# Final RMSNorm of a one-layer decoder: squares and norm weights handled per output block, last two blocks by token halves

## The reference

```python
def rmsnorm(x, g):
    xf = x.astype(jnp.float32)
    y = xf * lax.rsqrt(jnp.mean(xf * xf, axis=-1, keepdims=True) + EPS)
    return (y * g.astype(jnp.float32)).astype(x.dtype)
...
y = jnp.concatenate([ssm_out, att_out], axis=-1) @ w_out
...
y_prompt = rmsnorm(hp, g_final)[:, N_META:]
y_sample = rmsnorm(hs, g_final)
```

## Time and profile before

| what | value |
|---|---|
| median of 3 runs | 1257.17 us (1252.75 to 1259.44) |
| the profiled execution's own time | 1260.12 us |
| its span, first to last instruction | 1258.4 us |
| mean granted TensorE clock | 0.946 of full |
| busy: PE, DVE, ACT, POOL | 90%, 47%, 30%, 10% |
| last transpose of the projection ends | 1237.0 us |
| first write of `o_y_p` issued | 1244.1 us |
| write of `o_y_s` issued | 1255.6 us |

### The profile page before, as it was taken

How to read it: one execution, slowest core, us unless ns; L and a number is a source line. 1 busy time by engine, 2 the same in 40 slices (tenths; PEclk the granted TensorE clock), 3 DMA queues, 4 the chain that set the end, 5 groups by cost and what they waited for, 6 DMA issues and landing times.

```text
span 1258.4 us, 25162 instructions
## 1 busy us (share of the span) xinstructions
PE 1128.7 (90%) x9906; PEld 1032.3 (82%) x9906; DVE 585.2 (47%) x1205; ACT 375.0 (30%) x622; POOL 120.8 (10%) x192
## 2 busy tenths in 40 slices
PE   3899949999999999596989997799999988999993
PEld 3799949999999999586989975566666648999992
DVE  5843513442588521384646363455555462232224
ACT  6311101111233222335422213444444351121213
POOL 0000110000000000003405301022223100000000
PEclk8799969999999999698989898899999999999996
DMA  9343491332343532415437656166777728323203
GB/s 265 85 126 102 119 145 43 86 85 85 94 125 102 143 103 82 101 47 180 126 92 218 201 179 212 34 194 194 214 213 220 203 76 266 105 67 100 84 17 135
DMA packets 197187, 165.70 MB, mean 132 GB/s; under 512 B 35195, under 2 KB 163478, under 8 KB 195270
## 3 DMA queue, kind: packets, MB, share of 16 engines
q1 hardware_dynamic: 176358, 118.08, 33.4%
q0 software_dynamic: 9696, 27.04, 8.0%
q10 hardware_dynamic: 11048, 19.41, 4.6%
HBM read 139.36 MB, written 22.78 MB: 129 GB/s over the span
## 4 chain that ended last, share of the span: by engine, by line
PE 80%; DVE 6%; DMA 5%; ACT 3%; issue 3%; SPq 1%; POOL 0%; ACTq 0%; DVEq 0%
PE gemm L1758 13%; PE gemm L1760 13%; PE gemm L1759 13%; PE gemm L2084 5%; PE gemm L2086 4%; PE gemm L2085 4%; PE misc L1997 4%; PE gemm L2037 3%; PE gemm L2016 2%; DMA w_raw<-w_out 1%; PE misc L1834 1%; PE misc L1841 1%; PE misc L1983 1%; PE misc L1785 1%; PE gemm L1947 1%
## 5 line engine op out<-in xcount | busy, mean ns | idle before, releaser
L1758 PE MATMUL gemm<-xh,w_hi 128*128 128x260 f32 (+2 forms) x1120 | 321.9, 287 | 0.2 <-DVE w_lo L1152 0.2
L1760 PE MATMUL gemm<-xh,w_lo 128*128 128x260 f32 (+2 forms) x1120 | 319.8, 286 | 0.0
L1759 PE MATMUL gemm<-xl,w_hi 128*128 128x260 f32 (+2 forms) x1120 | 319.5, 285 | 0.0
L1152 DVE TENSOR_TENSOR w_lo<-w_raw,w_hi 128x2048 fp32r<-128x2048 f32 (+3 forms) x65 | 113.6, 1748 | 259.8 <-ACT w_hi L787 258.8
L1758 PEld LDWEIGHTS gemm<-xh,w_hi 128*128 128x128 f32 x1120 | 212.2, 189 | 1.1 <-DVE w_lo L1152 0.4
L1759 PEld LDWEIGHTS gemm<-xl,w_hi 128*128 128x128 f32 x1120 | 212.3, 190 | 0.0
L1760 PEld LDWEIGHTS gemm<-xh,w_lo 128*128 128x128 f32 x1120 | 212.1, 189 | 0.0
L787 ACT ACTIVATE w_hi<-w_raw 128x2048 fp32r<-128x2048 f32 (+3 forms) x63 | 90.7, 1439 | 354.7 <-PE gemm L1760 339.4
L2084 PE MATMUL gemm<-comb_hi,w_hi 128*128 128x260 f32 x512 | 147.4, 288 | 3.9 <-DVE w_lo L1642 2.9
L2086 PE MATMUL gemm<-comb_hi,w_lo 128*128 128x260 f32 x512 | 145.4, 284 | 0.0
L2085 PE MATMUL gemm<-comb_lo,w_hi 128*128 128x260 f32 x512 | 145.4, 284 | 0.0
(11 more groups left out here) (340 smaller groups left out, 1949.1 us busy)
## 6 DMA issues: line engine op xcount, KB each, us to landing
w_raw<-w_in SPq DMA_DIRECT2D x35, 1024.0 KB, 6.0
ckv<-cache_ckv POOLq DMA_DIRECT2D x72, 256.0 KB, 3.5
w_raw<-w_out SPq DMA_DIRECT2D x16, 1024.0 KB, 5.9
ckv<-cache_ckv SPq DMA_DIRECT2D x56, 256.0 KB, 2.9
z_d<-ev ACTq DMA_DIRECT2D x16, 260.0 KB, 2.1
w_raw<-w_glu SPq DMA_DIRECT2D x8, 512.0 KB, 4.4
yt<-x_prompt SPq DMA_DIRECT2D x4, 1024.0 KB
o_y_p<-yt SPq DMA_DIRECT2D x4, 1024.0 KB
```

The lines of the kernel that those rows point to most:

```text
L1152: dve.tensor_tensor(w_lo[:, slot, 0:width], w_raw[:, slot, 0:width], w_hi[:, slot, 0:width].bitcast(F32), ALU.subtract).then_inc(w_lo_read ...
L1758: pe.matmul(acc, a, xa, start=k == 0, stop=False)
L1759: pe.matmul(acc, a, xb, start=False, stop=False)
L1760: last = pe.matmul(acc, b, xa, start=False, stop=k == k_tiles - 1)
```

## The change

Five things are done:

1. Blocks 0 to 13: after a block is added, ACT squares its 128 columns in each of the five token tiles, each with an accumulated sum into a column of a new table `parts` (5 tiles by 16), and DVE then multiplies these columns of `yt` and `ysm` by their norm weights (`square_block`, `out_gain`). The sums are of the values ahead of the norm weights.
2. ACT takes a square root of a constant column ahead of the projection's copies.
3. Blocks 14 and 15 are multiplied, copied, turned and added by token halves, in the order 14 first half, (turn of block 13), 15 first half, 15 second half, 14 second half, with the turns of finished halves set between groups of contraction tiles.
4. The norm has two parts: token tiles 0 and 1 after the first halves of blocks 14 and 15 are added, under the second halves' matmuls; tiles 2, 3 and the sample tokens at the end. In a part ACT squares only the last 256 columns of each tile; DVE sums the 15 partial sums of its tiles in one instruction, and mean, root and reciprocal are made once for the part.
5. The scale goes onto the first 1792 columns, which hold their norm weights already, by a multiplication with one scalar per token: by ACT for tiles 1, 3 and the sample tokens (`y_scaled`), by DVE for 0 and 2. The last 256 columns are done as before, by scale and norm weights together. SP waits for both.

The diff, cut to its core:

```diff
@@ -204,6 +204,7 @@
         gfin = at("gfin", A0 + 57344, [P, D_MODEL])
         yb = at("yb", A0 + 65536, [P, 2, SEQ + N_SAMPLE])
         junk2 = at("junk2", A0 + 69696, [P, D_MODEL])
+        parts = at("parts", C0 + 1024, [P, 5, 16])
         oh = at("oh", A0, [P, 2, V_HEAD])
         zas = at("zas", A0 + 4096, [P, N_HEADS, N_SAMPLE])
         oz = at("oz", A0 + 4352, [P, N_HEADS, N_SAMPLE])
@@ -344,6 +345,7 @@
         out_t_ready = sem("out_t_ready")
         out_added = sem("out_added")
         y_stored = sem("y_stored")
+        y_scaled = sem("y_scaled")
         comb_hi_done = sem("comb_hi_done")
         comb_lo_done = sem("comb_lo_done")
 
@@ -404,6 +406,7 @@
         RING = len(ckv)
         S_BANK, SC, PVS, TP, PVB = (gemm[0], gemm[1]), gemm[2], gemm[3], misc[0], misc[1]
         T_BANK = (misc[2], misc[3])
+        MAIN = 14 * P
         EXTRA = slice(496, 512)
         NM, SM, SME, RS, PARTS = 24, 32, 40, 48, 56
 
@@ -690,10 +693,14 @@
                 for u in range(2):
                     sp.wait_ge(w_lo_ready, i * 2 + (B_OUT + 1 + u))
                     load_out(i * 2 + (2 + u), u)
+            o_y = d["o_y_p"].rearrange("b s m -> (b s) m")
             for t in range(4):
                 sp.wait_ge(x_scaled, t + 6)
-                sp.dma_start(d["o_y_p"].rearrange("b s m -> (b s) m")[t * P:(t + 1) * P, :], yt[:, t, :]).then_inc(y_stored, 16)
+                if t % 2:
+                    sp.wait_ge(y_scaled, t // 2 + 1)
+                sp.dma_start(o_y[t * P:(t + 1) * P, :], yt[:, t, :]).then_inc(y_stored, 16)
             sp.wait_ge(x_scaled, 10)
+            sp.wait_ge(y_scaled, 3)
             sp.dma_start(d["o_y_s"].rearrange("b s m -> (b s) m"), ysm[0:N_SAMPLE, :]).then_inc(y_stored, 16)
             sp.wait_ge(y_stored, 16 * 5)
 
@@ -1111,18 +1118,57 @@
 
             act.wait_ge(os_step, 6)
             act.activation(comb_hi[:, 8:16, T_PROMPT:T], oz[:], ACT.Copy).then_inc(os_step, 1)
-            with act.Fori(0, 7) as i:
+            act.activation(stat[:, 63:64], ident[:, 0:1], ACT.Sqrt)
+
+            def out_tile(t):
+                return (yt[:, t], P) if t < 4 else (ysm[0:N_SAMPLE], N_SAMPLE)
+
+            def squares(tiles, cols, width, col):
+                for t in tiles:
+                    y, rows = out_tile(t)
+                    last = act.activation(junk2[0:rows, t * 2 * P:t * 2 * P + width], y[:, cols], ACT.Square,
+                                          accum_out=parts[0:rows, t, col])
+                last.then_inc(x_squared, 1)
+
+            def square_block(j):
+                act.wait_ge(out_added, j + 3)
+                act.wait_ge(x_squared, j + 5)
+                squares(range(5), ds(j * P, P), P, ds(j, 1))
+
+            def out_copy_half(j, slot, h, done):
+                act.wait_ge(gemm_done, done)
+                act.wait_ge(out_t_ready, j + 1)
+                act.activation(yb[:, slot, h * 260:(h + 1) * 260], gemm[2 * slot + h][:, 0:260], ACT.Copy).then_inc(gemm_read, 1)
+
+            def finish(part, tiles, full):
+                act.wait_ge(out_added, 18 + 2 * part)
+                act.wait_ge(x_squared, 19 + part)
+                squares(tiles, slice(MAIN, D_MODEL), 2 * P, slice(14, 15))
+                act.wait_ge(var_ready, 8 + part)
+                act.activation(stat[:, 16:16 + len(tiles)], stat[:, 8:8 + len(tiles)], ACT.Sqrt).then_inc(std_ready, 1)
+                act.wait_ge(rstd_ready, 8 + part)
+                for t in full:
+                    y, rows = out_tile(t)
+                    at_t = 24 + t - tiles[0]
+                    act.activation(y[:, 0:MAIN], y[:, 0:MAIN], ACT.Copy, scale=stat[0:rows, at_t:at_t + 1]).then_inc(y_scaled, 1)
+
+            for u in range(2):
+                out_copy(u, u)
+                out_hi(2 + u, u, 1)
+            square_block(0)
+            with act.Fori(0, 6) as i:
                 for u in range(2):
-                    out_copy(i * 2 + u, u)
-                    out_hi(i * 2 + (2 + u), u, i + 1)
-            out_copy(14, 0)
-            out_copy(15, 1)
-            for t in range(5):
-                y, rows = (yt[:, t], P) if t < 4 else (ysm[0:N_SAMPLE], N_SAMPLE)
-                act.wait_ge(out_added, 18)
-                act.activation(junk2[0:rows], y, ACT.Square, accum_out=stat[0:rows, t:t + 1]).then_inc(x_squared, 1)
-                act.wait_ge(var_ready, t + 8)
-                act.activation(stat[0:rows, 16 + t:17 + t], stat[0:rows, 8 + t:9 + t], ACT.Sqrt).then_inc(std_ready, 1)
+                    out_copy(i * 2 + (2 + u), u)
+                    out_hi(i * 2 + (4 + u), u, i + 2)
+                    square_block(i * 2 + (1 + u))
+            DONE = B_V + 14
+            out_copy_half(14, 0, 0, DONE + 1)
+            square_block(13)
+            out_copy_half(15, 1, 0, DONE + 2)
+            finish(0, (0, 1), (1,))
+            out_copy_half(15, 1, 1, DONE + 3)
+            out_copy_half(14, 0, 1, DONE + 4)
+            finish(1, (2, 3, 4), (3, 4))
 
         @block.vector
         def _(dve):
@@ -1696,23 +1742,59 @@
             dve.wait_ge(os_step, 7)
             tt(comb_lo[:, 8:16, T_PROMPT:T], oz[:], comb_hi[:, 8:16, T_PROMPT:T].bitcast(F32), ALU.subtract).then_inc(os_step, 1)
 
+            dve.memset(parts[:], 1.0)
             dve.sem_inc(out_added, 2)
             dve.wait_ge(res_loaded, 16 * 6)
-            with dve.Fori(0, 7) as i:
+
+            def out_gain(j):
+                dve.wait_ge(x_squared, j + 6)
+                cols = yt[:, :, ds(j * P, P)]
+                tt(cols, cols, gfin[:, ds(j * P, P)].unsqueeze(1).to_broadcast([P, 4, P]), ALU.mult)
+                cols = ysm[0:N_SAMPLE, ds(j * P, P)]
+                tt(cols, cols, gfin[0:N_SAMPLE, ds(j * P, P)], ALU.mult)
+
+            def out_add_half(j, slot, h, turned):
+                dve.wait_ge(out_t_ready, turned)
+                cols = yt[:, 2 * h:2 * h + 2, j * P:(j + 1) * P]
+                last = tt(cols, cols, misc[slot][:, 2 * h * P:(2 * h + 2) * P].rearrange("p (t n) -> p t n", t=2), ALU.add)
+                if h:
+                    cols = ysm[0:N_SAMPLE, j * P:(j + 1) * P]
+                    last = tt(cols, cols, misc[2 + slot][0:N_SAMPLE, 0:P], ALU.add)
+                last.then_inc(out_added, 1)
+
+            def finish(part, tiles, full):
+                n = len(tiles)
+                dve.wait_ge(x_squared, 20 + part)
+                dve.reduce_sum(stat[:, 0:n], parts[:, tiles[0]:tiles[-1] + 1, 0:15], axis=AX.X).then_inc(comb_step, 1)
+                dve.wait_ge(comb_step, 9 + part)
+                dve.tensor_scalar(stat[:, 8:8 + n], stat[:, 0:n], 1.0 / D_MODEL, EPS, ALU.mult, ALU.add).then_inc(var_ready, 1)
+                dve.wait_ge(std_ready, 8 + part)
+                dve.reciprocal(stat[:, 24:24 + n], stat[:, 16:16 + n]).then_inc(rstd_ready, 1)
+                dve.wait_ge(rstd_ready, 8 + part)
+                for t in tiles:
+                    y, rows = (yt[:, t], P) if t < 4 else (ysm[0:N_SAMPLE], N_SAMPLE)
+                    scale_t = stat[0:rows, 24 + t - tiles[0]:25 + t - tiles[0]]
+                    if t in full:
+                        dve.tensor_scalar(y[:, 0:MAIN], y[:, 0:MAIN], scale_t, None, ALU.mult)
+                    dve.scalar_tensor_tensor(out=y[:, MAIN:D_MODEL], in0=y[:, MAIN:D_MODEL], scalar=scale_t, in1=gfin[0:rows, MAIN:D_MODEL],
+                                             op0=ALU.mult, op1=ALU.mult).then_inc(x_scaled, 1)
+
+            for u in range(2):
+                out_lo(2 + u, u)
+                out_add(u, u)
+            out_gain(0)
+            with dve.Fori(0, 6) as i:
                 for u in range(2):
-                    out_lo(i * 2 + (2 + u), u)
-                    out_add(i * 2 + u, u)
-            out_add(14, 0)
-            out_add(15, 1)
-            for t in range(5):
-                y, rows = (yt[:, t], P) if t < 4 else (ysm[0:N_SAMPLE], N_SAMPLE)
-                dve.wait_ge(x_squared, t + 6)
-                dve.tensor_scalar(stat[0:rows, 8 + t:9 + t], stat[0:rows, t:t + 1], 1.0 / D_MODEL, EPS, ALU.mult, ALU.add).then_inc(var_ready, 1)
-                dve.wait_ge(std_ready, t + 8)
-                dve.reciprocal(stat[0:rows, 24 + t:25 + t], stat[0:rows, 16 + t:17 + t]).then_inc(rstd_ready, 1)
-                dve.wait_ge(rstd_ready, t + 8)
-                dve.scalar_tensor_tensor(out=y, in0=y, scalar=stat[0:rows, 24 + t:25 + t], in1=gfin[0:rows],
-                                         op0=ALU.mult, op1=ALU.mult).then_inc(x_scaled, 1)
+                    out_lo(i * 2 + (4 + u), u)
+                    out_add(i * 2 + (2 + u), u)
+                    out_gain(i * 2 + (1 + u))
+            out_add_half(14, 0, 0, 17)
+            out_gain(13)
+            out_add_half(15, 1, 0, 18)
+            finish(0, (0, 1), (0,))
+            out_add_half(15, 1, 1, 19)
+            out_add_half(14, 0, 1, 20)
+            finish(1, (2, 3, 4), (2,))
 
         @block.tensor
         def _(pe):
```

(31 more changed lines are left out.)

## The result

| | kernel before | changed kernel |
|---|---|---|
| median, first comparison (11 runs each) | 1257.17 us | 1249.45 us (1245.53 to 1253.44) |
| ratio, 95% interval | | 0.9936, 0.9920 to 0.9952 |
| median, second comparison (11 and 8 runs) | 1257.56 us | 1249.60 us (1247.18 to 1255.17) |
| ratio, 95% interval | | 0.9924, 0.9908 to 0.9940 |
| span of the profiled execution | 1258.4 us | 1246.8 us |

By the ratios the changed kernel is faster by 0.64% and 0.76%, some 8 and 9.6 us; the medians differ by 7.7 and 8.0 us. The second lies clear of 0.995 too, while the first reaches 0.9952. The forecast was 1248.2, a ratio of 0.9929, in a range of 1244.5 to 1252.6.

What follows compares the result with a forecast made beforehand. PE held 80% of the chain, but mostly DVE the last 20.4 us. First end-part write 2.2 us earlier plus 6.8 less behind it: 9.0 off 1260.12, 1251.1; less 2.95 for the median, 1248.2; range 1244.5 to 1252.6.

Steps and rivals of the forecast that it cites:

- the tail: Stretch from the start of ACT's copy of block 13 to the end of the span; predicted 9.0 us less.
- Loop covered: Projection loop: added squares (1.9 us a block) and weight multiplications hide under matmuls; period stays 12.08 us.
- Halves give nothing by themselves in PE's order: Blocks 14 and 15: end part's squares begin at 1237.94 against 1237.97; the worth is what runs early.
- Part two: End norm of tiles 2, 3 and sample tokens: squares 1.46 us, reciprocal done 1240.27, tile 2 issued 1241.85.
- Writes: Last two large writes: 2.6 us per 1 MB after a 0.65 start, then 1.7 from last data to end.
- The slack of 1.6 us in part one: ACT is ready for its copy of block 15's second half early; 1.6 us remain before PE would wait.
- load 1.3: End chain: moving the table load ahead of the projection makes the first end-part write 1.3 us earlier.
- The rival in which the load stays: A table load ahead of a root in each norm part: 1.3 us more at the end, 1249.5; chance 0.07.
- drain of 1.38 us for each table switch: At the norm's table load: by the skill's drain 1.4 us more gain; left out, as the trace doesn't show it.
- rivals of a stall: PE waits for ACT in part one: stall plus 1.5 us of lost clock costs 4.4, giving 1252.6; chance 0.08.
- overrun loop: ACT's squares set the loop period: 13 blocks each lose 1.0 us and 1.5 by clock, about 1281; chance 0.03.
- the second rival: The overrun loop, where ACT's squares set the period and lost clock is added: about 1281; chance 0.03.

Runs made afterwards that it cites:

- late-ACT kernel: Changed kernel with two more squares of 1792 columns on ACT in part one, results unused; from block 13's copy to the end 39.11 us, 0.97 more.
- long fill: Changed kernel with idle ACT copies of 12288 columns in each of 12 loop periods; 14.23 us a period, 40.5 us from block 13's copy to the end.

## Why the prediction was right

The forecast held, and so did its mechanism: the tail was to shrink by 9.0 us and shrank by 8.81. That the medians agree so well is in part luck: whole times scatter by several us ahead of the tail, and the median of three runs that I started from, 1257.17, happens to be that of all eleven. Step by step, with times from the squares of the end part on:

- **Loop covered.** Shown: the period is unchanged, and unchanged with 4.4 us more on ACT (8.4 of 12.08 us); with 14.2 us of work ACT sets it. Where between these it turns wasn't measured. The squares took 1.56 us a block, not 1.9, since the next square overlaps the read before it.
- **Halves give nothing by themselves in PE's order.** Shown: squares at 26.58 us of the tail against 26.52. I had it at 26.49, 0.03 us earlier than before; of the 0.09 us missing, 0.07 are in PE's matmuls and early transposes and 0.02 in the copy, turn and add.
- **Part two.** Scaling begins after 2.22 us (predicted 2.33), tile 2 is issued after 3.79 (3.91), the sample rows after 5.76 (5.71). DVE's multiplication by one scalar took 1.15 us for 1792 columns, the low end of the bound and what the row's slope gave. ACT's took 1.79 against 1.68: the form that I took the slope from reads no scalar from SBUF. The late-ACT kernel's squares of 1792 columns, which read none either, took 1.68.
- **Writes.** From tile 2's issue to the end 7.77 us (predicted 7.55), at 397 to 422 GB/s. The last window makes 143 GB/s x 2.8 us = 0.40 MB behind 1244.0, about 0.95 us at 422 GB/s, so by this estimate it is 1.85 us from the last data to the end, where I took 1.7. Squares 0.09 later, issue 0.12 sooner behind them and writes 0.22 longer make the 0.19 us missing from 9.0.
- **The slack of 1.6 us in part one.** Measured 1.55. The late-ACT kernel used it up, and PE waited for the rest.

The step that was mis-sized is the load of the table, "load 1.3" in the list of steps. Alone it costs the end 1.04 us (the first root comes 1.09 earlier without it), since it covered DVE's mean, and in the changed kernel it needn't be moved ahead at all. The sum for part two had the mean in the chain already, which is why it came out. The rival in which the load stays was priced with a load in each part; even without the early root there is only one, in part one, and the tail is 0.07 longer.

The drain of 1.38 us for each table switch, which the Trainium skill states (ScalarE: Activation LUTs, What ACT_TABLE_LOAD costs), isn't in the traces: moving the load alone brought 1.04 us, and the root starts 0.01 to 0.02 us behind it.

The rivals of a stall and of an overrun loop were priced with a lost clock added to the wait. At the one wait of 0.88 us in part one the clock stayed at 1.00 and the cost was 0.97; a longer stall there wasn't tested. In the overrun loop the clock was lost behind one of the seven waits that fall in it, and the cost was still ACT's excess alone, 2.15 us a period: where another engine sets the pace, what the clock loses comes out of PE's next wait. That addition was the step that the second rival had wrong.

## What to carry to other kernels

A norm at the end of a kernel costs a chain per tile and then the writes: look at which would bound the end once the other is gone, since here the one cure alone was worth 2.9 us, the other 3.5, and both 8.8. Where a row's result is complete for some of the tokens earlier, finish and write those under the rest of the matmuls; what is left at the end should be judged by when its first write is issued and how many bytes follow. Compare single profiles from an event that both kernels share, as earlier stages may scatter by as much as the change is worth: here the copy of block 2 starts anywhere from 1073.5 to 1082.5 us.

## What the runs showed that I had not expected

The same wait for weights, at the same place in the same code, cost 19.2 to 23.6 us between the copies of blocks 0 and 2, according to whether the clock fell behind it. In six of the twelve traces it fell to 0.50 (waits of 2.1 to 2.9 us), and the stretch took 21.9 to 23.6 us; in the other six it stayed at 1.00 (waits of 1.0 to 2.7 us), and the stretch took 19.2 to 20.9. In the second profile of the changed kernel it was at 0.50 for some 6 us. The length of the wait doesn't decide it: 2.14 us lost the clock in one trace and 2.67 didn't in another. In the kernel with the long fill the same holds within one trace, where waits of 1.96 us left the clock alone twice and a later one of 1.82 didn't. What decides stays open.
